# Three groups of value projections moved behind gate projections, in a four-layer mixed attention program

## The reference

```
def even_layer(x, norm_g, w_in, b_f, gn_g, w_out):
    h = rms_norm(x, norm_g)
    u = h @ w_in
    q_f, k_f, v_f, f_l, q_r, k_r, v_r, z = jnp.split(u, EVEN_SPLITS, axis=-1)
    o_f = fox_attention(hd(q_f, FOX_HEADS), hd(k_f, FOX_HEADS), hd(v_f, FOX_HEADS), f_l + b_f)
    o_r = (retention(hd(q_r, RET_HEADS), hd(k_r, RET_HEADS), hd(v_r, RET_HEADS)) * gn_g).astype(x.dtype)
    y = jnp.concatenate([o_f, o_r], axis=-1) * jax.nn.silu(z)
    return x + y @ w_out
...
def odd_layer(x, norm_g, w_in, b_gate, pe_k, pe_v, wk1, wk2, wv1, wv2, w_out):
    h = rms_norm(x, norm_g)
    u = h @ w_in
    q, kc, vc, ks, vs, kw, vw, gl, z = jnp.split(u, ODD_SPLITS, axis=-1)
    o = nsa_attention(q.reshape(B, S, NSA_HEADS, HEAD_DIM), kv(kc), kv(vc), kv(ks), kv(vs), kv(kw), kv(vw),
                      gl, pe_k, pe_v, wk1, wk2, wv1, wv2)
    return x + (o * jax.nn.silu(z)) @ w_out
```

## Time and profile before

| | |
|---|---|
| median of 3 runs | 1565.15 us (1564.74 to 1565.19) |
| the profiled execution's own time | 1566.48 us |
| its span, first to last instruction | 1564.7 us |
| TensorE busy | 1476.0 us (94%) |
| VectorE busy | 973.4 us |
| ScalarE busy | 882.0 us |
| mean granted clock of TensorE | 0.981 |

### The profile page before, as it was taken

The page is one execution under the profiler, slowest core; times in us unless marked ns, Lnnn a source line. Parts: engine busy times, 40 slices in busy tenths (PEclk is TensorE's granted clock), DMA queues, the critical chain, the costliest instruction groups (busy, mean ns, idle before and its releaser), DMA issues.

```text
span 1564.7 us, 24980 instructions
## 1 busy us (share of the span) xinstructions
PE 1476.0 (94%) x10148; PEld 947.0 (61%) x10148; DVE 973.4 (62%) x1946; ACT 882.0 (56%) x1247; POOL 67.6 (4%) x148
## 2 busy tenths in 40 slices
PE   6999998999989999999998999989699999899997
PEld 3444485665458448585787666445385755466676
DVE  6732547888478566555667224576756336699974
ACT  4544456777554665454553453657354557678862
POOL 0000000000100100000010000001000000000000
PEclk8999999999999999999999999999899999999999
DMA  6233232111422334433325366411023332200002
GB/s 183 87 102 108 87 103 81 55 55 54 156 86 82 129 108 122 119 112 108 108 87 76 97 91 96 94 54 32 21 88 105 117 108 81 81 1 2 2 12 85
DMA packets 127218, 132.07 MB, mean 84 GB/s; under 512 B 9760, under 2 KB 124192, under 8 KB 126976
## 3 DMA queue, kind: packets, MB, share of 16 engines
q1 hardware_dynamic: 124336, 119.59, 27.0%
q0 software_dynamic: 2768, 10.89, 2.0%
HBM read 128.38 MB, written 2.10 MB: 83 GB/s over the span
## 4 chain that ended last, share of the span: by engine, by line
PE 59%; DVE 8%; ACT 4%; issue 2%; DMA 2%; POOL 0%; ACTq 0%; DVEq 0%
PE bank L709 8%; PE bank L710 8%; PE bank L711 8%; PE bank L748 6%; PE bank L750 5%; PE bank L749 5%; PE bank L942 3%; PE bank L924 3%; PE bank L915 2%; DVE wring L1872 2%; PE bank L911 1%; ACT whigh L1274 1%; DMA wring<-in_even_w_in 1%; PE bank L824 1%; DVE scr L2399 1%
## 5 line engine op out<-in xcount | busy, mean ns | idle before, releaser
L709 PE MATMUL bank<-xT,whigh 128*128 128x512 f16 x960 | 366.1, 381 | 10.4 <-DVE xT L2045 7.7
L710 PE MATMUL bank<-xT,whigh 128*128 128x512 f16 x960 | 366.0, 381 | 0.0
L711 PE MATMUL bank<-xT,wring 128*128 128x512 f16 x960 | 365.6, 381 | 0.0
L1872 DVE SCALAR_TENSOR_TENSOR wring<-wring,wsc,whigh 128x2048 f16<-128x2048 f32 x105 | 245.0, 2334 | 165.6 <-ACT whigh L1274 165.1
L1274 ACT ACTIVATE whigh<-wring,wsc 128x2048 f16<-128x2048 f32 x105 | 208.8, 1988 | 156.4 <-DVE wsc L1775 138.0
L1291 ACT ACTIVATE whigh<-wring 128x2048 bf16<-128x2048 f32 x105 | 199.0, 1895 | 121.3 <-DMA wring<-in_even_w_in 43.5
L748 PE MATMUL bank<-whigh,slab 128*128 128x256 f16 x800 | 218.0, 273 | 3.0 <-DVE wring L1872 1.2
L750 PE MATMUL bank<-whigh,slab 128*128 128x256 f16 x800 | 218.1, 273 | 0.0
L749 PE MATMUL bank<-wring,slab 128*128 128x256 f16 x800 | 218.0, 273 | 0.0
L709 PEld LDWEIGHTS bank<-xT,whigh 128*128 128x128 f16 x960 | 94.4, 98 | 126.3 <-DVE xT L2045 7.9
L711 PEld LDWEIGHTS bank<-xT,wring 128*128 128x128 f16 x960 | 94.4, 98 | 114.7 <-issue 2.5
(11 more groups left out here) (324 smaller groups left out, 2356.3 us busy)
## 6 DMA issues: line engine op xcount, KB each, us to landing
wring<-in_w_in SPq DMA_DIRECT2D x28, 1024.0 KB, 5.1
wring<-in_w_up SPq DMA_DIRECT2D x16, 1024.0 KB, 5.3
wring<-in_w_down SPq DMA_DIRECT2D x16, 1024.0 KB, 5.2
wring<-in_even_w_in SPq DMA_DIRECT2D x14, 1024.0 KB, 9.5
wring<-in_odd_w_in SPq DMA_DIRECT2D x14, 1024.0 KB, 4.9
wring<-in_w_a SPq DMA_DIRECT2D x4, 1024.0 KB, 5.2
wring<-in_w_out SPq DMA_DIRECT2D x4, 1024.0 KB, 5.2
wring<-in_even_w_out SPq DMA_DIRECT2D x4, 1024.0 KB, 4.7
```

The source lines that it names most:

```text
L709: pe.matmul(bank, wh[:, k, wcol:wcol + width], xh[:, k, :], start=k == 0, stop=False)
L710: pe.matmul(bank, wh[:, k, wcol:wcol + width], xl[:, k, :], start=False, stop=False)
L711: mm = pe.matmul(bank, wl[:, k, wcol:wcol + width], xh[:, k, :], start=False, stop=k == KC - 1)
L1872: dve.scalar_tensor_tensor(low_of(i)[:, :, 0:m], loaded(i)[:, :, 0:m], wsc[:, n:n + 1], high_of(i)[:, :, 0:m], ALU.mult, ALU.subtract).the ...
```

## The change

It moves three groups of value projections on TensorE, with what belongs to them on the other engines.

- In `stream`, `ze` comes ahead of `vr`, and `vw` comes behind `zo`, not between `cv0` and `cv1`.
- The first two score steps of an attention (`EARLY`) come right behind the gates. Then come value tiles 0 and 1 of the first `vr` slot (or of `vw`), the third step, value tiles 2 and 3, and the other steps. `ze` uses the other four banks, its sigmoids other rows of `scr`.
- The second `vr` slot's four tiles stand between retention's score groups ("pieces"). These now alternate between two pairs of banks, and the orders of retention on TensorE, ScalarE and VectorE are written out by hand. Mean, variance and result use other banks.
- The preparation calls (`period`, `following`, `before`, `after`) go with their slots: `oe` slot 0 is now measured after FOX's third step, and its halves are made ahead of step 6; `oe` slot 1 is measured in retention.
- `gated_scale` moves from step 2 to step 6 (FOX) and step 9 (NSA). For NSA the maximum over `vw`'s values is taken behind the third step.
- The transposed probabilities of FOX and retention's buffer are in `slab[3]`, since `xT` is still wanted by `vr`.

The core of the diff:

```diff
         add("kr", W, 2056, 512)
+        add("ze", W, 3080, 1024)
         add("vr", W, 2568, 512, 4)
-        add("ze", W, 3080, 1024)
...
         add("vs", W, 1792, 256, 4)
         first_layer("v", 0)
-        add("vw", W, 2304, 256, 4)
         first_layer("v", 1)
...
             stream.append(("qo", cols(W, SLOTW * i), SLOTW, 2 * i + 2))
         add("zo", W, 2608, 1024)
+        add("vw", W, 2304, 256, 4)
...
-        def turned_probs(i, e):
-            return xT[:, 2 * (i % TURNED_SLOTS) + e, :]
+        def turned_probs(A, i, e):
+            return (slab[3] if A.name == "fox" else xT)[:, 2 * (i % TURNED_SLOTS) + e, :]
...
-                    if n == split_index(name, 2):
+                    if n == split_index(name, {"oe": 0, "oo": 2}[name]):
                         pool.wait_ge(s_("out_max"), OUTS.index(name) + 1)
...
+            def retention_values(w, tiles):
+
+                for n in tiles:
+                    if n >= 6:
+                        pe.wait_ge(s_("vr_ev"), n_("vr_ev", n - 1))
+                    tok_tile("vr", w, n % 4, xhalves, RBANKS[n][:, 0:SLOTW])
...
+                def pieces(m, groups):
+
+                    for group in groups:
+                        q = 3 * m + group
+                        if q >= 2:
+                            pe.wait_ge(s_("rt_ea"), q - 1)
+                        for j in RET_GROUPS[group]:
...
+                w = slot("vr")
+                pieces(0, (0, 1))
+                retention_values(w, (4,))
+                pieces(0, (2,))
+                pieces(1, (0,))
+                retention_values(w, (5,))
+                values(0)
+                pieces(1, (1,))
+                retention_values(w, (6,))
+                pieces(1, (2,))
+                means(0)
+                retention_values(w, (7,))
+                values(1)
+                variances(0)
+                pieces(2, (0, 1))
+                means(1)
+                pieces(2, (2,))
+                variances(1)
+                pieces(3, (0,))
+                values(2)
+                pieces(3, (1, 2))
+                means(2)
+                values(3)
+                variances(2)
                 means(3)
                 return lambda: variances(3)
...
-            tok("vr", 2, xhalves, SB)
+            feat("ze", 8, xhalves, SB)
             pe.wait_ge(s_("kr_ev"), n_("kr_ev", 4))
-            feat("ze", 8, xhalves, SA)
-            pe.wait_ge(s_("ze_ev"), n_("ze_ev", 8))
-            pe.wait_ge(s_("vr_ev"), n_("vr_ev", 8))
             pe.wait_ge(s_("frow_both"), 1)
             pe.wait_ge(s_("decay_in"), 32)
-            attention(FOX)
+            attention(FOX, EARLY)
+            w = slot("vr")
+            pe.wait_ge(s_("ze_ev"), n_("ze_ev", 8))
+            retention_values(w, (0, 1))
+            attention(FOX, FOX.later[0:1])
+            retention_values(w, (2, 3))
+            attention(FOX, FOX.later[1:])
             pe.wait_ge(s_("fox_y"), 4)
...
+                tok("gl", 1, xhalves, [SA[0][:, P * t:P * t + P] for t in range(TT)], width=48)
+
             pe.wait_ge(s_("kw_ev"), n_("kw_ev", 2))
             pe.wait_ge(s_("kw_half"), 2)
             pe.wait_ge(s_("vs_ev"), n_("vs_ev", 4))
-            tok("vw", 1, xhalves, VBANKS[1])
-            first_layer(1, 1)
...
-            pe.wait_ge(s_("zo_ev"), n_("zo_ev", 8))
-            pe.wait_ge(s_("ct_ev"), 16)
             pe.wait_ge(s_("ks_ev"), n_("ks_ev", 2))
             pe.wait_ge(s_("ks_half"), 2)
-            pe.wait_ge(s_("kw_ev"), n_("kw_ev", 2))
-            pe.wait_ge(s_("kw_half"), 2)
-            attention(NSA)
+            attention(NSA, EARLY)
+            w = slot("vw")
+            pe.wait_ge(s_("zo_ev"), n_("zo_ev", 8))
+            window_values(w, (0, 1))
+            attention(NSA, NSA.later[0:1])
+            pe.wait_ge(s_("ct_ev"), 16)
+            window_values(w, (2, 3))
+            attention(NSA, NSA.later[1:])
...
+            for m in range(8):
+                if m % 2 == 0:
+                    period("ze", m // 2)
+                act.wait_ge(s_("ze_mm"), n_("ze_mm", m + 1))
+                if m >= 2:
+                    act.wait_ge(s_("ze_ev"), n_("ze_ev", m - 1))
+                act.activation(scr[:, 4 + m % 2, :], SB[m % 4][:, :], ACT.Sigmoid, scale=undo("ze", m // 2)).then_inc(s_("ze_sg"), 1)
+                act.wait_ge(s_("ze_sg"), own(s_("ze_sg")))
+                if m % 2 == 0:
+                    following("ze", m // 2)
+
+            def retention_values(tiles):
+
+                for n in tiles:
+                    s, t = divmod(n, TT)
+                    ev("vr", n, vtok[:, t, 512 + s * SLOTW:512 + (s + 1) * SLOTW], bank=RBANKS[n][:, 0:SLOTW], scale=undo("vr", s))
+
+            period("vr", 0)
             act.wait_ge(s_("ze_ev"), n_("ze_ev", 8))
-            attention(FOX)
-
-            def ret_copies(m):
-
-                for group, js in enumerate(RET_GROUPS):
+            attention(FOX, EARLY)
+            retention_values((0, 1))
+            following("vr", 0)
+            attention(FOX, FOX.later[0:1])
+            retention_values((2, 3))
+            attention(FOX, FOX.later[1:4])
+            period("vr", 1)
...
+
+            ret_copy(0, 0, 1)
+            retention_values((4,))
+            ret_copy(0, 2)
+            ret_copy(1, 0)
+            retention_values((5,))
+            following("vr", 1)
+            pair_out_copy(0)
+            ret_copy(1, 1)
+            retention_values((6,))
+            ret_copy(1, 2)
+            pair_square(0)
+            retention_values((7,))
+            ret_copy(2, 0, 1)
+            pair_out_copy(1)
+            pair_root(0)
+            ret_copy(2, 2)
+            pair_square(1)
+            ret_copy(3, 0)
+            pair_root(1)
+            ret_copy(3, 1, 2)
+            pair_out_copy(2)
+            out_high("oe", 4, slab[5][:, 4, :], "yr", 1)
+            pair_square(2)
+            pair_out_copy(3)
+            pair_root(2)
...
             act.activation(kcmp, SA[2][:, 0:NG * NC], ACT.Copy).then_inc(s_("cmp_ev"), 1)
             act.wait_ge(s_("cmp_ev"), own(s_("cmp_ev")))
-            for t in range(TT):
-                if t == 3:
-                    period("cv1")
-                ev("vw", t, vtok[:, t, 256:512], bank=VBANKS[1][t][:, 0:256], scale=undo("vw", 0))
-                if t == 1:
-                    following("vw")
+            following("cv0")
+            period("cv1")
...
+            period("vw")
+            attention(NSA, EARLY)
+            window_values((0, 1))
+            attention(NSA, NSA.later[0:1])
+            window_values((2, 3))
+            following("vw")
+            attention(NSA, NSA.later[1:])
...
+                    if name == "ze":
+                        last.then_inc(s_("out_max"), 1)
 
...
+                early = slice(first, first + (1 if name == "oe" else 2))
+                dve.tensor_scalar(winv[:, early], winv[:, early], xinv[:, c], None, ALU.mult).then_inc(dve_chain, 1)
...
-                    if i == 2:
+                    if i == {"fox": 6, "nsa": 9}[n]:
...
+            def behind_even_gate(m):
+
+                if m >= 1:
+                    bound_behind("ze", m - 1)
+
+            silu("ze", slab[5], SB, {m: lambda m=m: behind_even_gate(m) for m in range(8)})
+            bound_behind("ze", 7)
+
+            before("vr", 0)
+            attention(FOX, EARLY)
+            attention(FOX, FOX.later[0:1])
+            after("vr", 0)
+            attention(FOX, FOX.later[1:4])
+            before("vr", 1)
+            attention(FOX, FOX.later[4:])
...
+            ret_mask(0, 0, 1, 2)
+            ret_mask(1, 0)
+            after("vr", 1)
+            ret_mask(1, 1, 2)
+            ret_centre(0)
+            ret_mask(2, 0, 1)
+            ret_finish(0)
+            ret_centre(1)
+            ret_mask(2, 2)
+            ret_mask(3, 0)
+            ret_finish(1)
+            ret_mask(3, 1, 2)
+            ret_centre(2)
             out_low("oe", 4, slab[5][:, 4, :])
-            retention_out(2)
+            ret_finish(2)
             out_low("oe", 5, slab[5][:, 5, :])
             norm_bound("rms_o")
             out_low("oe", 6, slab[5][:, 6, :])
-            retention_out(3)
+            ret_centre(3)
+            ret_finish(3)
             out_low("oe", 7, slab[5][:, 7, :])
             add_and_norm("oe", SA, 1.0, None, "rms_o", normed, SB, "kc")
...
             before("cv0")
-            after("vw")
+            after("cv0")
             before("cv1")
...
-            attention(NSA)
+            before("vw")
+            attention(NSA, EARLY)
+            attention(NSA, NSA.later[0:1])
+            dve.wait_ge(s_("vw_ev"), n_("vw_ev", 4))
+            dve.tensor_reduce(hmax[:, 1, 0:1], vtok[:, :, 256:512], mybir.AxisListType.XY, ALU.max, apply_absolute_value=True).then_inc(dve_chain, 1)
+            dve.wait_ge(dve_chain, own(dve_chain))
```

(3 more changed lines are left out.)

147 lines of the change are left out of this document (58 added, 89 removed), and 4 rows, old and new, of the table counted.

## The result

The changed kernel takes 1585.3 us (1584.1 to 1588.1), the one before beside it 1565.0 us (1564.7 to 1565.2): ratio 1.0132, 95% interval 1.0115 to 1.0150, so 20 us slower. The profiled execution spans 1584.6 us, before 1564.7. The forecast was 1578, with eight chances in ten for 1564 to 1585: the direction is right, the sum is 7 us too small.

The account below looks back on a forecast made before the run. TensorE, busy 94% of the span, was taken as the bound: its work plus its gaps. Terms -2.3 + 3.9 + 2.6 + 1.0 + 5.7 + 2.3 + 0 = +13.2 us on 1565.15 gave 1578 us; eight in ten, 1564 to 1585.

Parts of the forecast that it names:

- the clock's term: Half clock behind PE stands: 1.0 us lost in retention, 2.3 us lost at the first queries.
- Part 1: First attention's start: tiles fill some gaps despite a 4.4 us stand; 2.3 us gained (3.1 gained to 0.7 lost).
- part 2: Middle of first attention: splits and `gated_scale` ahead of step 6's softmax make PE wait; 3.9 us lost (0 to 6).
- Part 3: Retention: later reciprocals and output lose 2.6 us, half clock 1.0 more; ends 10.4 gained to 5.5 lost.
- Part 4: Before the first queries: query slot ready late, 5.7 us lost (5.3 to 6.2), plus half clock 2.3 (0 to 3).
- rival (c): First queries: query slot is ready in time, 8 us off the sum, 1570 us; chance 5%.
- Part 5: Second attention: 1.9 us gained at its start, later waits cancel it; 0 together (3 gained to 1.5 lost).
- Rival (a): Attention starts and retention: fills work without holding a softmax or root; -18.7 us, 1546 us; chance 10%.
- Rival (b): Only query wait and mid-attention stall are real, retention ties, starts fill half; +1.4 us, 1567 us; chance 15%.

Follow-up runs that it names:

- experiment 3: Changed kernel with the low and high halves ahead of both attentions' first steps moved behind the first two steps: 1583.6 us, ratio 1.0100 to the kernel before.
- experiment 4: Changed kernel with the output projection's first-slot split moved from the middle of the first attention to its end: 1583.5 us, ratio 1.0090 to the kernel before.
- experiment 7: Changed kernel with retention's roots ahead of the copies and its last two value tiles moved to where TensorE stands: 1577.0 us, ratio 1.0063 to the kernel before.
- experiment 9: Changed kernel with unread filler matmuls at five TensorE stands (third score steps, retention's mean and variance, first queries): 1577.2 us, ratio 1.0065 to the kernel before.
- experiment 6: Changed kernel with ScalarE's square roots ahead of the score copies in retention: 1584.5 us, ratio 1.0104 to the kernel before.
- experiment 2: Kernel before with only the odd layer's part of the change: 1575.3 us, ratio 1.0041 to the kernel before.
- experiment 8: Changed kernel, odd layer as before, with late low half, no mid-attention split, roots first and last two tiles in retention's holes: 1559.5 us, ratio 0.9946 to before.
- experiment 10: Kernel before with filler matmuls before both third score steps and ahead of the even output: 1570.4 us, ratio 1.0020 to the kernel before.
- experiment 12: Whole change, odd part kept, with late low halves in both layers, output split behind the first attention, last two tiles in retention's holes: 1566.9 us, ratio 0.9994.
- the better order: Kernel of experiment 8, ratio 0.9946 to the kernel before; with filler at the even output and the odd attention's third step 1557.7 us, ratio 0.9946.

## Why the prediction came out too low

**The direction and the waits were right.** The reading was that PE's gaps are not filled but made by the in-order lists of VectorE and ScalarE, and that splits would move ahead of softmax operations. The stands: 4.33 us predicted as 4.4, 3.80 as 3.9, retention's two 3.80 and 3.79 as 3.7 and 4.4, 5.61 as 5.7, 3.50 as 4.5. Experiments 3, 4 and 7 take three of the causes away one by one and the stand goes with it each time.

**The step that failed** is the clock's term in parts 1 and 2. Part 1 carried half clock only as an end of its range ("a loss of 0.7 if the 4.4 us stand brings half clock"), part 2 not at all. Both stands brought it: 4.8 us and 5.8 us at 0.50, about 2.4 and 2.8 us. I had taken the one stand of 3.49 us without half clock behind it as the nearest row for part 1, where the earlier trace rows had two of about 4.2 us with it. So part 1 is +0.2 instead of -2.3 and part 2 +6.7 instead of +3.9: 5.3 of the 6.8 us by which the sum (+13.2 against +20.0) was short. For part 1 the price is measured: with the stand filled (experiment 9) the fifth step comes 22.5 us after the gates, the prediction's 22.6, in place of 25.1. For part 2 it is inferred. Experiment 4 removes wait and half clock together, 6.7 us in that stretch against a wait of 3.80; in experiment 3 the clock behind the same wait was low for a shorter time, and the stretch was 1.2 us shorter.

Other rows of before spoke against the exception too. A third stand, of only 3.21 us, had the half clock behind it (inside the 26 us of the earlier trace rows, at 0.50 here):

```profile
1099.23 2.08 PE L979 MATMUL bank<-scr,half_mean 128*128 128x512 f32 x2 [3.21 <-ACT scr L1621]
```

```profile
1099.20:1105.40 6.20, 5.30 (x8) 0.50 0.00 0
```

The range failed with it: the terms' own upper ends add up to more than the measured +20 (0.7 + 6 + 5.5 + 6.2 + 3 + 1.5 = 22.9), but they were taken as partly independent, and the half clock came behind every new stand of the profile.

**Part 3** was mis-sized the same way. The first reciprocal starts 28.3 us after the scores (predicted 27.5), the output comes at 55.4 (52.5 + 1.0 predicted). Behind the two stands the clock was at 0.61 and 0.52 for 11.7 us. Experiment 9 gives its price: with both filled the first reciprocal is at 28.3 again and the output at 53.5, so 1.9 us where the sum had 1.0; the rest is the later first reciprocal. The 5.5 us that retention lost is the upper end that part 3 stated for half clock behind both stands. That ScalarE's order makes the first root late is only a small part (experiment 6: 0.9 us); the tiles' place ahead of the first variance is the main one (experiment 7: another 7.8 us). I named both and gave no weights.

**Part 4.** The wait was 5.61 for 5.7, by the chain as told, so rival (c), a query slot ready in time, is out. The half clock behind it came (4.6 us at 0.50), yet the stretch up to the gates' end was not longer than before. The kernel before had lost as much clock there, with PE busy throughout and no stand ahead of it:

```profile
1323.90:1327.30 3.40, 3.40 (x13) 0.50 0.00 0
1340.90:1344.30 3.40, 3.40 (x11) 0.50 0.02 5
```

The stretch up to the queries is longer by 1.4 us more than the wait. PE began the even output projection at half clock for longer than the 3.5 us of the earlier trace rows (first row below), but that makes only 0.4 us by 1182.8, and the next 12 us are 0.7 shorter than before. Most of the 1.4 is one group of 48 matmuls behind it (`L834` to `L836`), which took 4.2 us in place of 2.7 at a lowered clock (second row):

```profile
1129.20:1134.00 4.80, 4.66 (x19) 0.50 0.00 0
```

```profile
1194.60:1198.80 4.20, 4.18 (x49) 0.63 0.01 4
```

Both deviations look like chance of one pair of profiles. Taken over the profiles of all the kernels here without filling at the queries, the stretch from the first queries to the gates' end averages 110.5 us (108.9 to 112.4) in the seven that have the change's odd part and 107.8 (106.3 to 109.2) in the five that don't: +2.7 for a term of 2.3. The stretch from the output to the first queries averages 131.4 and 136.2, which with the tiles' 10.4 makes +5.6 for 5.7. So both terms of part 4 were right as far as this shows, and that they come to 1.1 us less in the table is luck.

**Part 5** was 0 and measured -0.2, from -2.8 and +2.6 where I had -1.9 and +1.9.

**The Trainium skill's rule** ("TensorE: Matmul & The Clock Gate", Part 1: the throttled state is the default and idling leads back to it) would have given 16 by the prediction's own working; applied to part 2 as well, 16 + 2.8 = 18.8 as an estimate, near the 20 measured. Experiment 9 agrees with it: full clock behind five filled stands, half clock behind the unfilled one.

Idling does not account for the two rows of 3.40 us above, at half clock with PE busy throughout.

The exception in the trace of before, the 3.49 us stand, should not have carried the sum. In experiment 2 this part is untouched, and the same wait for the same 3.49 us was followed by a lowered clock:

```profile
1035.80:1039.20 3.40, 0.00 (x0) 1.00 0.00 0
1039.20:1041.50 2.30, 2.25 (x18) 0.70 0.00 0
1041.50:1046.00 4.50, 4.44 (x20) 0.77 0.00 2
```

It cost nothing there: the fifth score step came 14.5 us after the gates, as before, because the wait of 1.75 us ahead of it went away in turn. The half clock has its price where PE would otherwise not have waited.

**Rival (a), that the fills work,** was wrong for the order the change has and right for the idea: experiment 8 gains 8 us from the even half. Rival (b) (the fills cost and give nothing, 1567) left out the clock as I did. Why filling stands pays in the change and not in the kernel before is shown for one place only, the second attention's start (experiment 10), where the next wait grows by what PE gained; that ScalarE and VectorE set the pace there in general is argued from this, not shown. Not settled is by what the single executions of one kernel differ by up to 8 us. The place in experiment 4 and the two 3.49 us stands say that the clock has a part in it, and so do experiment 12's eleven executions (mean clock 0.985 in the fastest, 1562.0 us; 0.980 in the slowest, 1570.0 us); the kernel before shows no such order (0.980 at 1564.0, 0.982 at 1570.1).

## What to carry to other kernels

A gap of the busiest engine can be filled only at the spot where its instruction stands in the list: work put a few microseconds ahead of the hole delays the chain that makes it, and the hole stays (experiment 7 against experiment 6: 6 to 8 us for moving two tiles by a few positions). When work moves, look first at what goes with it into the other engines' in-order queues; here two splits ahead of softmax operations cost more than the tiles in retention (by their stretches about 5 and 6.7 us in experiments 3 and 4, against 7.8). And a new stand of TensorE like these (3.5 to 5.6 us) goes into the sum with the half clock behind it, about 2.5 us where dense work follows and nothing where PE would have waited again anyway. One row without it is no evidence that a stand is free. Before explaining a difference of 1 or 2 us between two profiles, compare the same stretch over several (part 4).

## What the runs showed of the hardware

- Behind stands of 3.5 to 5.6 us TensorE worked at 1.2 GHz for about 5 us; keeping it busy with matmuls that nobody reads kept it at 2.4 GHz behind every filled place (experiment 9), worth 6.9 us of 1585 by the stretches of three of them, in a kernel that was 8 to 10 us faster. I had not expected useless work to pay.
- In the kernel before, the same trick cost 0.2%, and in the better order it gave nothing: the next wait grew instead.
- The clock also fell with TensorE busy throughout: 0.50 for 3.4 us from 1323.9 and from 1340.9 in the kernel before, both times within 1 us behind 32 small matmuls (`L1039`, 64x31). The same 32 matmuls at 1283.4 and 1296.2 had no such fall behind them; what makes the difference is open.
- Stands of the same length do not always bring the same: the two of 3.49 us above; and 3.80 us before 1049.7 was followed by 0.50 for 5.8 us, and the stand of 3.81 us before 1044.5 in experiment 3 by 0.66 over 5 us.
